# A transformer block on one core: the norm's factors inside x's first transfer, and a new order of accumulating transfers for the down product

## The reference

```
h    = rmsnorm(x, g_pre_mix)
proj = h @ w_in        # q, k, v of two attentions, the indexer's q, k and head weights, two gates
o_a  = sparse attention (indexer scores, top 128 keys, softmax with a relative bias)
o_b  = stick-breaking attention
m    = sigmoid(gate_a) * (o_a @ w_branch_sparse) + sigmoid(gate_b) * (o_b @ w_branch_sb)
x    = x + rmsnorm(m @ w_out, g_post_mix)
h    = rmsnorm(x, g_pre_ffn)
g, u = split(h @ w_gate_up)                       # 2816 channels each
x    = x + rmsnorm((silu(g) * u) @ w_down, g_post_ffn)
```

## Time and profile before

| what | value |
|---|---|
| median of 3 runs | 736.43 us (736.42 to 737.09) |
| the profiled execution, its own time | 736.68 us |
| its span, first to last instruction | 734.9 us |
| PE busy | 728.3 us (99%) |
| DVE, ACT, POOL busy | 596.7, 466.4, 260.5 us |
| transfers | 95.21 MB, mean 130 GB/s |

### The profile page before, as it was taken

The page is one execution under the profiler, slowest core; times in us unless marked ns, Lnnn a source line. Parts: engine busy times, 40 slices in busy tenths (PEclk is TensorE's granted clock), DMA queues, the critical chain, the costliest instruction groups (busy, mean ns, idle before and its releaser), DMA issues.

```text
span 734.9 us, 11111 instructions
## 1 busy us (share of the span) xinstructions
PE 728.3 (99%) x3867; PEld 627.4 (85%) x3867; DVE 596.7 (81%) x843; ACT 466.4 (63%) x733; POOL 260.5 (35%) x204
## 2 busy tenths in 40 slices
PE   9999999999999999999999999999999999999997
PEld 8788888888888888888888999999999999887885
DVE  4989989978866767359998888888888888995787
ACT  5663177777758676654485756666766666764664
POOL 4697265876777878421103400000000000043201
PEclk9999999999999999999999999999999999999999
DMA  9662444222404223268971023333333344999914
GB/s 333 191 181 65 147 120 115 57 58 59 113 9 130 65 71 111 62 185 273 280 188 34 1 83 93 111 114 114 115 113 87 93 163 157 343 174 206 213 37 116
DMA packets 111488, 95.21 MB, mean 130 GB/s; under 512 B 3664, under 2 KB 91736, under 8 KB 111448
## 3 DMA queue, kind: packets, MB, share of 16 engines
q1 hardware_dynamic: 104920, 78.96, 34.6%
q0 software_dynamic: 6368, 15.73, 11.6%
q10 hardware_dynamic: 160, 0.01, 0.0%
HBM read 84.97 MB, written 4.73 MB: 122 GB/s over the span
## 4 chain that ended last, share of the span: by engine, by line
PE 94%; DVE 2%; DMA 2%; issue 1%; ACT 1%; POOL 0%; POOLq 0%; DVEq 0%; ACTq 0%
PE ps L1048 13%; PE ps L710 11%; PE ps L711 11%; PE ps L712 11%; PE ps L1129 9%; PE ps L1054 6%; PE ps L732 6%; PE ps L971 4%; PE ps L777 3%; PE ps L1036 3%; PE ps L1038 3%; PE ps L1037 3%; PE ps L928 3%; PE ps L917 2%; DMA w_a<-in_w_down 2%; PE ps L991 1%
## 5 line engine op out<-in xcount | busy, mean ns | idle before, releaser
L710 PE MATMUL ps<-h_both,w_hi 128*128 128x512 f32 (+1 forms) x288 | 110.4, 383 | 0.0
L711 PE MATMUL ps<-h_both,w_hi 128*128 128x512 f32 (+1 forms) x288 | 109.1, 379 | 0.0
L712 PE MATMUL ps<-h_both,w_lo 128*128 128x512 f32 (+1 forms) x288 | 109.0, 379 | 0.0
L1919 POOL DMA_DIRECT2D w_a<-in_w_down x12 | 15.3, 1531 | 249.6 <-DMA w_a<-in_w_down 227.1
L1833 POOL TENSOR_TENSOR w_lo<-raw,w_hi 128x1024 fp32r<-128x1024 f32 x30 | 76.0, 2537 | 31.0 <-ACT w_hi L1320 30.6
L712 PEld LDWEIGHTS ps<-h_both,w_lo 128*128 128x128 f32 x288 | 54.2, 188 | 10.3
L710 PEld LDWEIGHTS ps<-h_both,w_hi 128*128 128x128 f32 x288 | 54.2, 188 | 9.1
L711 PEld LDWEIGHTS ps<-h_both,w_hi 128*128 128x128 f32 x288 | 54.3, 189 | 9.0
L2471 DVE TENSOR_TENSOR wr_lo<-w_a,wr_hi 128x1536 fp32r<-128x1536 f32 (+1 forms) x28 | 45.4, 1622 | 18.9 <-ACT wr_hi L1635 18.8
L1129 PE MATMUL ps<-wr_hi,xd_hi 128*128 128x512 f32 x154 | 60.1, 390 | 0.2 <-DVE xd_lo L2476 0.2
L1129 PE MATMUL ps<-wr_lo,xd_hi 128*128 128x512 f32 x154 | 60.0, 389 | 0.0
(11 more groups left out here) (328 smaller groups left out, 2076.7 us busy)
## 6 DMA issues: line engine op xcount, KB each, us to landing
raw<-in_w_in SPq DMA_DIRECT2D x40, 512.0 KB, 4.6
raw<-in_w_gate_up SPq DMA_DIRECT2D x24, 512.0 KB, 3.8
raw<-in_w_gate_up SPq DMA_DIRECT2D x40, 256.0 KB, 4.2
w_a<-in_w_down SPq DMA_DIRECT2D x9, 768.0 KB, 6.2
w_a<-in_w_down POOLq DMA_DIRECT2D x9, 768.0 KB, 10.6
s<-in_w_out SPq DMA_DIRECT2D x3, 768.0 KB, 7.7
w_a<-w_a POOLq DMA_DIRECT2D x3, 768.0 KB, 13.2
x_t<-in_first SPq DMA_DIRECT2D x8, 256.0 KB, 6.5
```

The source lines that it names most:

```text
L710: mm(acc, whi_c, a_hi_, start=first, stop=False, skip_group_check=further)
L711: mm(acc, whi_c, a_lo_, start=False, stop=False, skip_group_check=further)
L712: return mm(acc, wlo_c, a_hi_, start=False, stop=last, skip_group_check=further)
```

## The change

The kernel gets an array `first_x` [128, 520] in place of `gain_cols`: x's first chunk with the 8 columns of factors behind it. It lands in a new tile `x_first`, in memory that nothing uses at that time. `g_cols` is now the end of that tile, chunk 0 of x its beginning. The first weights are issued by ACT, where the transfer of `g_cols` was, and ACT's wait for `g_cols` is gone. In the down product POOL's order and the thresholds for k = 3 and 5 change for groups 2 and 3; no transfer is added or removed there.

```diff
@@ build
-    g_cols = sb("g_cols", KC)
+    top[0] = ki_at - 4 * 3 * S
+    x_first = sb("x_first", S + KC)
+    top[0] = ki_at
+    g_cols = x_first[:, S:S + KC]
+
+    def x_of(c):
+        return x_t[:, c, :] if c else x_first[:, 0:S]
@@ sync
         def x_chunk_in(c):
-            sp.dma_start(x_t[:, c, :], first[c, :, 0:S]).then_inc(x_t_in[c], 16)
+            if c:
+                sp.dma_start(x_t[:, c, :], first[c, :, 0:S]).then_inc(x_t_in[c], 16)
+            else:
+                sp.dma_start(x_first[:, :], first_x).then_inc(x_t_in[0], 16)
...
         for c in range(TB + 1):
             x_chunk_in(c)
-            wq_chunk_in(c)
+            if c:
+                wq_chunk_in(c)
@@ scalar
-            run(xg_hi[:, c, :], x_t[:, c, :], ACT.Copy, scale=g_cols[:, c:c + 1]).then_inc(xg_hi_done, 1)
+            run(xg_hi[:, c, :], x_of(c), ACT.Copy, scale=g_cols[:, c:c + 1]).then_inc(xg_hi_done, 1)
...
-        sc.dma_start(g_cols[:, :], gain_cols).then_inc(g_cols_in, 16)
+        sc.dma_start(wq_raw[:, 0, :], first[0, :, S:2 * S]).then_inc(wq_in[0], 16)
         sc.dma_start(rel_t[:, :], rel_cols).then_inc(small_in, 16)
         nc.scalar.preload_act_table(ACT.Sqrt)
         sc.sem_inc(acc_free, PAIRS)
-        sc.wait_ge(g_cols_in, 16)
         round_x(0)
...
-                sc.wait_ge(block_added[g], {5: 32, 3: 48, 4: 64, 6: 80}[k])
+                sc.wait_ge(block_added[g], {5: 32 if g < 2 else 48, 3: 48 if g < 2 else 32, 4: 64, 6: 80}[k])
@@ gpsimd
-        def added(nth, dst, src, split_before):
-            for g in range(4):
+        def added(nth, dst, src, split_before, groups=range(4)):
+            for g in groups:
                 gp.wait_ge(parts_lo_done, UP_PARTS + 4 * split_before + g + 1)
                 if nth:
                     gp.wait_ge(block_added[g], 16 * nth + 16)
...
-        added(0, w_a11, lambda g: w_group(1, 0, g), 0)
-        added(1, w_a22, lambda g: w_group(1, 0, g), 2)
+        added(0, w_a11, lambda g: w_group(1, 0, g), 0, range(2))
+        added(1, w_a22, lambda g: w_group(1, 0, g), 2, range(2))
+        added(0, w_a22, lambda g: w_group(1, 0, g), 2, range(2, 4))
+        added(1, w_a11, lambda g: w_group(1, 0, g), 0, range(2, 4))
         added(2, w_a22, lambda g: w_group(0, 0, g), 3)
         added(3, w_a12, lambda g: group_of(w_a22, g), 1)
@@ vector: rest_x and make_h read x_of(c) for x_t[:, c, :]
```

More of the change, by code:

```diff
@@ L132, in bias_runs, with build @@
     return runs
-def build(nc, first, gain_cols, first_kw, rel_cols, x, w_in, w_branch_sparse, w_branch_sb, w_out, w_gate_up, w_down,
+def build(nc, first, first_x, first_kw, rel_cols, x, w_in, w_branch_sparse, w_branch_sb, w_out, w_gate_up, w_down,
           g_pre_mix, g_post_mix, g_pre_ffn, g_post_ffn, out):
@@ L392, in build @@
     x_rows_in = sems(*(f"x_rows_in{t}" for t in range(TB)))
-    small_in, kw_in, g_cols_in = sems("small_in", "kw_in", "g_cols_in")
+    small_in, kw_in = sems("small_in", "kw_in")
     x_t_in, wq_in = sems(*(f"x_t_in{c}" for c in range(KC))), sems(*(f"wq_in{c}" for c in range(KC)))
@@ L1965, in rest_x @@
             ve.wait_ge(xg_hi_done, c + 1)
-            stt(xg_lo[:, c, :], x_t[:, c, :], g_cols[:, c:c + 1], xg_hi[:, c, :], ALU.mult, sub).then_inc(xg_lo_done, 1)
+            stt(xg_lo[:, c, :], x_of(c), g_cols[:, c:c + 1], xg_hi[:, c, :], ALU.mult, sub).then_inc(xg_lo_done, 1)
         def make_h(c):
@@ L1970, in make_h @@
                 ve.wait_ge(xh_lo_done, c - 1)
-            stt(bank(4 + c % 2), x_t[:, c, :], g_cols[:, c:c + 1], bank(7), ALU.mult, ALU.mult).then_inc(xh_made, 1)
+            stt(bank(4 + c % 2), x_of(c), g_cols[:, c:c + 1], bank(7), ALU.mult, ALU.mult).then_inc(xh_made, 1)
         def rest_h(c):
@@ L2547 @@
     laid = {"first": np.concatenate([np.asarray(inputs["x"][0]).T, w[:, COL_QI:COL_QI + W]], axis=1).reshape(KC, P, 2 * S),
-            "gain_cols": np.asarray(inputs["g_pre_mix"][0]).reshape(KC, P).T,
+            "first_x": np.concatenate([np.asarray(inputs["x"][0]).T[0:P], np.asarray(inputs["g_pre_mix"][0]).reshape(KC, P).T],
+                                      axis=1),
             "first_kw": w[:, COL_KI:COL_KI + KW].reshape(KC, P, KW).transpose(1, 0, 2).reshape(P, KC * KW),
```

## The result

The change made the kernel slower: 741.03 us (median of 6 runs, 740.32 to 741.15) against 736.5 (6 runs), a ratio of 1.0055 with a 95% interval of 1.0044 to 1.0065. The forecast was 736.6, in a range of 735.8 to 737.6. The profiled execution took 740.92 us with a span of 739.0, 4.1 more than the span before.

A forecast was written before the change was run, and what follows sets the result against it. The prediction took TensorE's fixed stream of matmuls, busy 99% of the span, as the bound. Opening +0.1, old stall -0.48 and new stall +0.5 gave +0.1, so 736.6 us against the median, range 735.8 to 737.6.

The forecast's parts named there:

- the old stall: TensorE's wait in the fourth product's first groups for the weights' accumulating transfer; the reordering would remove it, -0.48 us.
- the new stall: TensorE's wait before the fifth product's first group, near 684 us, for its late transfer; forecast +0.5 us.
- The opening's transfers: x and the first weights share the engines; x lands between 3.45 and 4.10, TensorE 0 to 0.4 us late, costing 0.1.
- full restart at each late issue: GpSimd's queue: w_a11's late groups land as into an idle queue (7.6 us for 768 KB), the fifth product's first at 681.3.
- the unevenness: The 1.0 us by which the same nine transfers exceeded the queue's pace before; added to 681.3 it gives 682.3.
- half of 679.3 to 681.3: 680.3: Forecast landing of the fifth product's first transfer, midway between no holes in GpSimd's queue and full restarts.
- The landings of the fourth product: Its four accumulating weight transfers on GpSimd's queue were forecast to land at 659.4, 663.5, 667.3 and 669.8 us.
- Rival (3): Fifth product: full restarts and the same unevenness, landing at 682.3, a stall of 2.5, 738.6 us; chance 0.05.
- Rival (4): Opening: a gap before the first real matmul delays the clock's rise by 4.8 us, costing 2.2, 738.7 us; chance 0.04.
- The chance of slower: Forecast chance that the whole kernel measures slower, beyond the 0.2% (1.5 us) that the measurement tells: 0.09.

The follow-up runs named there:

- the opening alone: Only the change's first part (merged factors, first weights issued by ACT), down product in the old order, against the kernel before: 736.77 us, ratio 1.0002.
- the order alone: Only the down product's new transfer order and thresholds, opening as before, against the kernel before: 741.83 us, ratio 1.0068.
- the first run with a semaphore of its own: New order, old opening, w_a11's groups 2 and 3 counted on a separate semaphore, so issued without waiting for w_a22's landings: 739.32 us, ratio 1.0033.
- the two runs with such a semaphore: Old opening, separate semaphore for w_a11's groups behind the fourth product's transfers: groups 2 and 3, 739.32 us; only group 3, 736.43 us.
- filling the gap: New order with old opening, plus 12 matmuls with zeros on TensorE ahead of the fifth product: 739.9 us, ratio 1.0043 to the kernel before.
- the run with the fifth product first: New order with old opening, but w_a11's groups 2 and 3 issued behind all the fifth product's transfers: 736.3 us, ratio 0.999 to the kernel before.
- the run without a hole: Old opening, only w_a11's group 3 behind the fourth product's transfers, on a separate semaphore: 736.43 us, ratio 0.9994 to the kernel before.

## Why the prediction was wrong

**Right.** TensorE bounds the kernel, and the old stall went, as ScalarE's starts show; it was worth 0.58 us where 0.48 had been summed (its three terms give 0.47), since the slower matmuls around it were not all counted. The place of the new stall, its cause (w_a11's late groups, their turned landing wait, GpSimd standing in it) and the issue times of the fourth product were as forecast. The opening's transfers did land together and late, x at about 4.5 and the weights at about 4.7, beyond the 4.10 that was taken as the worst: x's chunk 1 shared the engines from 1.20 us on, which the forecast didn't count and whose part no run shows. TensorE's first real weight load was 0.7 us late, more than the 0.4 of the forecast, yet the opening alone measured as before.

**The step that failed is the landing of the fifth product's first transfer.** The prediction worked out 681.3 with a full restart at each late issue and 682.3 with the unevenness, then took "half of 679.3 to 681.3: 680.3", because each issue comes with one transfer in flight. It came at 682.6, 2.3 later. The argument for the half does not hold for this queue. With w_a11's group 1 in flight until 654.6, the issue at 651.95 took 7.6 us to land, as into an idle queue, and left the flow at 91 GB/s until 656; the issue at 668.81, with w_a22's group 3 in flight until 670.8, took 7.3. By the traces the landing waits were worth 1.6 us of delay (the order alone against the first run with a semaphore of its own), and the early hole with the slower flow behind it 2.4 (the two runs with such a semaphore).

The half was also at odds with the rest of the sum. The landings of the fourth product, 659.4 to 669.8, held the first restart in full and were right to about 1 us; by them the pace alone brings the fifth product's first to 669.8 + 3.83 + 2.52 + 3.83 = 680.0, so 679.3 was no longer open as a lower bound. And the 1.0 us of unevenness was in 679.3 but not in 681.3. Rival (3), given 0.05, had both restarts and the unevenness: it put the landing at 682.3 and the stall at 2.5 us, and 682.6 and 2.84 were measured. A smaller term was missing too: between a landing (670.8 in the chain) and the issue behind it (671.32) lies half a microsecond.

**The term that no case held is the clock behind the new stall.** Rival (4) priced the slow level only for the opening, where the gap was at most 0.4 us by the forecast. In the down product the stall of 2.84 us cost 1.75 more, and filling the gap won 1.6 of such a loss back. With that term, and the stall as measured, rival (3) would have given 736.43 + 0.1 - 0.48 + 2.84 + 1.75 = 740.6. The Trainium skill, TensorE: Matmul & The Clock Gate, Part 1, which rival (4) cites, says that idle time returns the throttle; the trace agrees, with 0.53 behind the stall. The prediction weighed this for the opening's gap only, and not for the stall that it forecast in the down product.

**The chance of slower** was 0.09 because each seam was judged by itself against 0.5 us of slack. The slack was smaller than the price of one restart (7.6 us from issue to landing for 768 KB, against 3.8 in the flow), which the rows had shown.

## What to carry to other kernels

When transfers are reordered in a queue that is the bound of its stretch, ask first where the queue runs dry: an issue that waits, or a landing that the next issue waits for, can cost the start-up again, here even with a transfer still in flight. Put what is needed last behind everything that is needed sooner, and not merely behind the one product that waits now. And price a TensorE stall of some microseconds at more than its length, because the matmuls behind it may run at half the clock.

## What the runs showed of the hardware

- The clock stood at 1.2 GHz behind two matmul starts 3.07 us apart (granted 0.53 over the next 3.5 us), and not behind two 1.94 us apart. In the order alone, with starts 3.53 us apart, the slow spacing began only 1.0 us behind the stall's end. The first group behind the stall took 5.8 us in both, against 4.08.
- In the opening the rise to 2.4 GHz comes at another time in each execution of the same code: the spacing goes from 0.43 to 0.23 us at about 5.9 in the trace of before, and between 6.6 and 6.9 in the run with the fifth product first, whose opening is the same. The first down group begins at 624.01 and 624.40, so this is part of the spread between runs of one kernel. In the timeline of PEld of that run four weight loads take 1.15 us where they took 0.87 before:

```profile
6.14 1.15 PEld L777 LDWEIGHTS ps<-xg_lo,wq_hi 128*128 128x128 f32 x4
```

- An accumulating transfer that is issued late, with the one before it still in flight, leaves the queue below its pace of 205 GB/s for about 3 us (issue at 651.95, the one before landed at 654.6, 91 GB/s from 653 to 656). Behind such a hole the flow stays lower: from 657 to 668 us it was 198 GB/s in the change, 184 and 191 in two of the runs with the same hole, and 204 and 203 in before and in the run without a hole.
